# The chunk inversion of an RWKV-7 layer on 32x32 diagonal blocks in four partition quadrants, with one joining level

## The reference, cut to what matters

```python
def rwkv7_scan(r, w, k, v, kk, a, s0):
    def step(s, inp):
        r_t, w_t, k_t, v_t, kk_t, a_t = inp
        s_kk = jnp.einsum('bhvk,bhk->bhv', s, kk_t)
        s = (s * w_t[:, :, None, :] - s_kk[..., None] * (kk_t * a_t)[:, :, None, :]
             + v_t[..., None] * k_t[:, :, None, :])
        return s, jnp.einsum('bhvk,bhk->bhv', s, r_t)
```

## Time and profile before

| | |
|---|---|
| median of 3 runs | 4778.01 us (4769.5 to 4778.93) |
| the profiled execution | 4774.47 us |
| its span, first to last instruction | 4772.8 us |
| mean granted TensorE clock | 0.923 of 2.4 GHz |
| RWKV layers, inversion and chain | 371 to 998 us and 3829 to 4441 us |

### The profile page before, as it was taken

The page is one execution under the profiler, slowest core; times in us unless marked ns, Lnnn a source line. Parts: engine busy times, 40 slices in busy tenths (PEclk is TensorE's granted clock), DMA queues, the critical chain, the costliest instruction groups (busy, mean ns, idle before and its releaser), DMA issues.

```text
span 4772.8 us, 95942 instructions
## 1 busy us (share of the span) xinstructions
PE 4178.3 (88%) x37843; PEld 2571.5 (54%) x37843; DVE 2314.5 (48%) x4411; ACT 1370.2 (29%) x2518; POOL 525.5 (11%) x523
## 2 busy tenths in 40 slices
PE   4797999979999899978999885789997979999797
PEld 4346878844444344433444344444443468888676
DVE  5555555436652466633664215366623145555331
ACT  1004555421210355521221014222201045554230
POOL 0002323200000122210000000000000023232000
PEclk6898999989999899989999997899998979999899
DMA  4330000014432223213443210144421200000243
GB/s 147 97 117 26 4 4 4 3 40 135 148 116 86 69 91 95 89 44 101 141 141 101 71 59 0 35 127 141 128 84 54 83 19 3 4 4 4 83 133 109
DMA packets 475026, 350.75 MB, mean 73 GB/s; under 512 B 18016, under 2 KB 443176, under 8 KB 472520
## 3 DMA queue, kind: packets, MB, share of 16 engines
q1 hardware_dynamic: 449784, 240.11, 17.2%
q0 software_dynamic: 24912, 105.87, 6.2%
HBM read 344.76 MB, written 1.18 MB: 72 GB/s over the span
## 4 chain that ended last, share of the span: by engine, by line
PE 73%; DVE 13%; ACT 6%; issue 4%; DMA 4%; SPq 0%; DVEq 0%; ACTq 0%; POOLq 0%
PE PS L225 50%; PE PS L1417 18%; DMA WR<-in_ffn_w_in_dram 2%; PE PS L348 2%; DVE WORK L450 1%; DVE WORK L341 1%; DVE WORK L1169 1%; DVE WORK L1172 1%; DVE WORK L780 1%; PE PS L949 1%; DMA WR<-in_ffn_w_out_dram 1%; DVE H L453 1%; ACT WORK L1057 1%; ACT WORK L1654 0%; DVE BIG L1864 0%
## 5 line engine op out<-in xcount | busy, mean ns | idle before, releaser
L225 PE MATMUL PS<-H,WR 128*128 128x512 f32 (+1 forms) x3792 | 1519.5, 560 | 100.2 <-DVE WORK L540 37.8
L225 PEld LDWEIGHTS PS<-H,WR 128*128 128x128 f32 x3792 | 718.5, 192 | 859.4 <-issue 791.2
L225 PE MATMUL PS<-BIG,WR 128*128 128x512 f32 (+1 forms) x2592 | 1043.9, 564 | 92.8 <-DVE BIG L1818 59.2
L225 PEld LDWEIGHTS PS<-BIG,WR 128*128 128x128 f32 x2592 | 498.7, 194 | 625.5 <-issue 593.9
L341 DVE SCALAR_TENSOR_TENSOR WORK<-WORK,SC 128x512 f32<-128x512 f32 (+2 forms) x798 | 487.9, 611 | 28.5
L1417 PE MATMUL PS<-BIG,WORK 64*64 64x32 f32 (+1 forms) x9984 | 438.3, 224 | 61.4 <-DVE BIG L1924 60.0
L1417 PE MATMUL PS<-WORK,BIG 64*64 64x32 f32 (+1 forms) x8960 | 452.3, 227 | 23.8 <-DVE WORK L1928 12.9
L1417 PEld LDWEIGHTS PS<-BIG,WORK 64*64 64x64 f32 x9984 | 374.6, 140 | 90.2 <-issue 65.1
L1417 PEld LDWEIGHTS PS<-WORK,BIG 64*64 64x64 f32 x8960 | 370.9, 142 | 81.7 <-ACT WORK L1643 29.6
L579 DVE SCALAR_TENSOR_TENSOR X<-PS,MOD,X 128x256 f32 x112 | 54.2, 484 | 607.3 <-PE PS L225 598.4
L1772 POOL TENSOR_TENSOR WORK<-WORK,K 128x256 f32<-128x256 f32 x320 | 255.0, 797 | 788.4 <-ACT WORK L1643 396.9
(11 more groups left out here) (237 smaller groups left out, 4298.4 us busy)
## 6 DMA issues: line engine op xcount, KB each, us to landing
WR<-in_ffn_w_in_dram SPq DMA_DIRECT2D x176, 512.0 KB, 3.7
WORK<-in_ada_w_dram POOLq DMA_DIRECT2D x33, 2048.0 KB, 8.6
WR<-in_ffn_w_out_dram SPq DMA_DIRECT2D x64, 512.0 KB, 3.9
WR<-in_ssd_w_in_dram SPq DMA_DIRECT2D x48, 512.0 KB, 3.9
BIG<-scratch_dram POOLq DMA_DIRECT2D x8, 2048.0 KB, 7.9
BIG<-in_ada_w_dram SPq DMA_DIRECT2D x6, 2048.0 KB, 8.0
WORK<-in_ada_w_dram POOLq DMA_DIRECT2D x12, 1024.0 KB, 5.9
WR<-in_ffn_w_out_dram SPq DMA_DIRECT2D x32, 384.0 KB, 3.3
```

What stands on the lines that cost most here:

```text
L225: mm = pe.matmul(outs, WR[:, slot, k, 0:m], rhs(k), start=first and k == 0, stop=last and k == nk - 1)
```

## The change

The 64x64 matrix is first inverted on its two 32x32 diagonal blocks alone, and these lie one below the other on partitions: `QUADS[b][n]` is block b of head n, so four quadrants of 32 partitions hold two heads times two blocks. A matmul has 32 weight rows and 32 weight columns there and serves one quadrant, one chunk. `YX` holds both forms of the four chunks of one thread, 32 columns each; `NS` gets the off-diagonal 32x32 block of the product as well, which G makes on its own (10 matmuls a chunk in place of 4). The levels 2 to 16 run as before on these blocks: Z has 16 matmuls of 32 columns, X 32 of 16 columns.

A fifth step pair, m = `LAST`, joins the blocks. Z multiplies the off-diagonal block with the natural form of one diagonal block, with weights in one quadrant and the result in the other. X writes the whole 64x64 natural inverse into PSUM: both diagonal blocks by multiplying the transposed form with the identity, the off-diagonal one with Z, 24 matmuls, 8 of them of 64 columns. One VectorE copy of 256 columns takes it to `INV`, which no longer has a transposed form. The masks on GpSimd are four, of 128 columns, and the identity on ScalarE is written at the start of the own slot, since `YX` is shared by the thread before. Matmuls of the inversion: 8192 before, 16896 after; the chain, R, H and everything outside the RWKV layers stay.

```diff
-LEVELS = (2, 4, 8, 16, 32)
+LEVELS = (2, 4, 8, 16)
...
-HALF_CONST = ["id64", "id64", "pair0", "pair1", "lev2_0", "lev2_1", "lev4_0", "lev4_1", "lev8_0", "lev8_1",
-              "lev16_0", "lev16_1", "lev32_0", "lev32_1"]
+HALF_CONST = ["id64"]
+QUARTER_CONST = ["id32", "pair0", "pair1"] + [f"lev{n}_{d}" for n in (2, 4, 8, 16) for d in range(2)]
...
-        INV = work(4 * T).rearrange("p (d h c f) -> p d h c f", d=2, h=2, c=NQ)
-        G2, BK, G1R = by_chunk(P), by_chunk(P), by_chunk(Q)
+        INV, G2, BK, G1R = by_chunk(Q), by_chunk(P), by_chunk(P), by_chunk(Q)
+        YX = work(8 * Q).rearrange("p (d h c f) -> p d h c f", d=2, h=2, c=4)
         VTK = [work(T) for _ in range(2)]
-        sub = lambda: work(4 * Q).rearrange("p (c f) -> p c f", c=4)
-        NS = [sub() for _ in range(2)]
+        NS = [work(4 * Q).rearrange("p (o c f) -> p o c f", o=2, c=4) for _ in range(2)]
+        sub = lambda: work(4 * 32).rearrange("p (c f) -> p c f", c=4)
         OM = [[sub() for _ in range(2)] for _ in range(2)]
         ZB = [sub() for _ in range(2)]
-        ZB32 = [z[:, 0:2, :].rearrange("p c (h f) -> p (c h) f", h=2) for z in ZB]
         SIG, AA, RESET, PN = both_d(T), both_d(T), work(T), both_d(T)
         ARS = work(2048).rearrange("p (d n t) -> p d n t", d=2, n=2)
...
+        QUADS = [[slice(Q * n + 32 * b, Q * n + 32 * b + 32) for n in range(2)] for b in range(2)]
+        LAST = len(LEVELS)
...
-            for m in range(len(LEVELS)):
+            for m in range(LAST + 1):
                 inv += [(k, q, s, m) for k in "ZX" for q in both]
...
-            if h + 1 < SLOTS:
-                beside += [(22 + d, "I", 2 * ((h + 1) // 2) + d, (h + 1) % 2) for d in range(2)]
-            steps = [("I", d, 0) for d in range(2)] if h == 0 else []
+            steps = [("I", q, s) for q in both]
...
                 bank, removed = PS[:, 3 + d, :], AR[i % 2][:, d, 0, :]
+                half = lambda c, b: slice(ORDER_Q[d][4 * s + c] * Q + 32 * b, ORDER_Q[d][4 * s + c] * Q + 32 * b + 32)
                 for c in range(4):
-                    cs = tok(ORDER_Q[d][4 * s + c])
-                    for hs in HALF:
-                        last = mm(bank[hs, 4 * Q + c * Q:4 * Q + c * Q + Q], removed[hs, cs], AD[hs, d, cs])
-                done(last, f"{q}.gt{s}")
-                for c in range(4):
-                    cs = tok(ORDER_Q[d][4 * s + c])
-                    for hs in HALF:
-                        last = mm(bank[hs, c * Q:c * Q + Q], AD[hs, d, cs], removed[hs, cs])
+                    for b in range(2):
+                        for n, hs in enumerate(HALF):
+                            mm(bank[QUADS[b][n], c * 32:c * 32 + 32], AD[hs, d, half(c, b)], removed[hs, half(c, b)])
+                    for b in range(2):
+                        for n, hs in enumerate(HALF):
+                            mm(bank[QUADS[b][n], 256 + c * 32:256 + c * 32 + 32], removed[hs, half(c, b)], AD[hs, d, half(c, b)])
+                    b = 1 - d
+                    for n, hs in enumerate(HALF):
+                        last = mm(bank[QUADS[b][n], 384 + c * 32:384 + c * 32 + 32], removed[hs, half(c, b)],
+                                  AD[hs, d, half(c, 1 - b)])
                 done(last, f"{q}.g1{s}")
...
             def z_step(q, s, m):
-                d, n = q % 2, LEVELS[m]
-                pe.wait_ge(pool_done, C.at(f"{t}.{q}.om{s}{m}"))
+                d = q % 2
                 pe.wait_ge(vec_done, C.at(f"{t}.{q}.xx{s}{m - 1}") if m else C.at(f"{t}.{q}.xi{s}"))
+                if m < LAST:
+                    pe.wait_ge(pool_done, C.at(f"{t}.{q}.om{s}{m}"))
                 for c in range(4):
-                    y = INV[:, d, 0, 4 * s + c, :]
-                    o = slice(c * Q, c * Q + Q) if n < 32 else slice(c * 32, c * 32 + 32)
-                    for hs in HALF:
-                        last = mm(PS[hs, 3 + d, o], OM[d][m % 2][hs, c, :],
-                                  y[hs, :] if n < 32 else y[hs, 32 - 32 * d:64 - 32 * d])
+                    o = slice(c * 32, c * 32 + 32)
+                    if m < LAST:
+                        for b in range(2):
+                            for qs in QUADS[b]:
+                                last = mm(PS[qs, 3 + d, o], OM[d][m % 2][qs, c, :], YX[qs, d, 0, c, :])
+                    else:
+                        for to, qs in zip(QUADS[d], QUADS[1 - d]):
+                            last = mm(PS[to, 3 + d, o], NS[d][qs, 1, c, :], YX[qs, d, 0, c, :])
                 done(last, f"{q}.z{s}{m}")
 
             def x_step(q, s, m):
-                d, n = q % 2, LEVELS[m]
+                d = q % 2
                 pe.wait_ge(act_done, C.at(f"{t}.{q}.zc{s}{m}"))
-                bank = PS[:, 3 + d, 4 * Q:]
+                bank = PS[:, 3 + d, :]
+                if m == LAST:
+                    for c in range(4):
+                        o = 256 + c * Q
+                        for qs, own in zip(QUADS[d], QUADS[1 - d]):
+                            mm(bank[qs, o + 32 * d:o + 32 * d + 32], YX[qs, d, 1, c, :], quarter_const("id32")[qs, :])
+                            mm(bank[own, o:o + Q], YX[own, d, 1, c, :], half_const("id64")[own, :])
+                        for qs in QUADS[d]:
+                            last = mm(bank[qs, o + 32 - 32 * d:o + 64 - 32 * d], YX[qs, d, 1, c, :], ZB[d][qs, c, :])
+                    done(last, f"{q}.x{s}{m}")
+                    return
+                n = LEVELS[m]
                 for c in range(4):
-                    for hs in HALF:
-                        z = second(d, n)(ZB[d][hs, c, :]) if n < 32 else ZB32[d][hs, c, :]
-                        out = bank[hs, c * 32:c * 32 + 32]
-                        last = mm(blocks_of(out, n) if n < 32 else out, INV[hs, d, 1, 4 * s + c, :], z)
-                done(last, f"{q}.xy{s}{m}")
-                if n < 32:
-                    for c in range(4):
-                        for hs in HALF:
-                            last = mm(blocks_of(bank[hs, P + c * 32:P + c * 32 + 32], n), ZB[d][hs, c, :],
-                                      first(d, n)(INV[hs, d, 1, 4 * s + c, :]))
-                    done(last, f"{q}.x{s}{m}")
+                    for b in range(2):
+                        for qs in QUADS[b]:
+                            last = mm(blocks_of(bank[qs, P + c * 16:P + c * 16 + 16], n), YX[qs, d, 1, c, :],
+                                      second(d, n)(ZB[d][qs, c, :]))
+                for c in range(4):
+                    for b in range(2):
+                        for qs in QUADS[b]:
+                            last = mm(blocks_of(bank[qs, 192 + c * 16:192 + c * 16 + 16], n), ZB[d][qs, c, :],
+                                      first(d, n)(YX[qs, d, 1, c, :]))
+                done(last, f"{q}.x{s}{m}")
...
             def identity(q, s_):
-                if q >= 2:
-                    act.wait_ge(pe_done, C.at(f"{t}.{q - 2}.u{4 * s_ + 3}"))
-                eye = half_const("id64").unsqueeze(1).unsqueeze(1).broadcast_to([P, 2, 4, Q])
-                s(act.activation(INV[:, q % 2, :, 4 * s_:4 * s_ + 4, :], eye, ACT.Copy), f"{t}.{q}.id{s_}")
+                if q >= 2 or s_:
+                    q0, s0 = thread_before(q, s_)
+                    act.wait_ge(pe_done, C.at(f"{t}.{q0}.x{s0}{LAST}"))
+                eye = quarter_const("id32").unsqueeze(1).broadcast_to([P, 8, 32])
...
-                    act.wait_ge(pool_done, C.at(f"{t}.{q0}.om{s0}{len(LEVELS) - 1}"))
-                copy(NS[q % 2].rearrange("p c f -> p (c f)"), PS[:, 3 + q % 2, 4 * Q:], f"{q}.n{s_}")
+                    act.wait_ge(pe_done, C.at(f"{t}.{q0}.z{s0}{LAST}"))
+                copy(NS[q % 2].rearrange("p o c f -> p (o c f)"), PS[:, 3 + q % 2, 4 * Q:], f"{q}.n{s_}")
...
-                cols = 4 * Q if LEVELS[m] < 32 else 4 * 32
-                copy(ZB[q % 2].rearrange("p c f -> p (c f)")[:, 0:cols], PS[:, 3 + q % 2, 0:cols], f"{q}.zc{s_}{m}")
+                copy(ZB[q % 2].rearrange("p c f -> p (c f)"), PS[:, 3 + q % 2, 0:P], f"{q}.zc{s_}{m}")
...
-                lev = half_const(f"lev{LEVELS[m]}_{q % 2}").unsqueeze(1).broadcast_to([P, 4, Q])
-                g(pool.tensor_tensor(OM[q % 2][m % 2], NS[q % 2], lev, ALU.mult), f"{t}.{q}.om{s_}{m}")
+                lev = quarter_const(f"lev{LEVELS[m]}_{q % 2}").unsqueeze(1).broadcast_to([P, 4, 32])
+                g(pool.tensor_tensor(OM[q % 2][m % 2], NS[q % 2][:, 0, :, :], lev, ALU.mult), f"{t}.{q}.om{s_}{m}")
...
-                pair = lambda n: by4(half_const(f"pair{n}")).bitcast(mybir.dt.int32)
+                pair = lambda n: by4(quarter_const(f"pair{n}")).bitcast(mybir.dt.int32)
                 c4 = lambda ap: ap.rearrange("p (c f) -> p c f", c=4)
                 vec.wait_ge(act_done, C.at(f"{t}.{q}.n{s_}"))
-                v(vec.copy_predicated(half_inv(q, s_, 0), pair(d), c4(PS[:, 3 + d, 0:4 * Q])))
```

(22 more changed lines are left out.)

22 lines of the change are left out of this document (15 added, 7 removed).

## The result

| | before | after |
|---|---|---|
| median | 4773.8 us (4 runs) | 5030.9 us (5027.3 to 5041.2, 4 runs) |
| ratio | | 1.0542, 95% interval 1.052 to 1.0563 |
| span of the profiled execution | 4772.8 us | 5025.6 us |
| instruction packets (queue q8) | 252 | 388 |

The changed kernel is 257 us slower. The forecast was +52 us (4830), in the range but far from its middle; the cause of most of the loss was in none of its terms.

What follows compares the result with a forecast made beforehand. It took the RWKV layers to be bound by TensorE's rate of small matmuls, priced by weight loads. Matmuls -152, shape changes +164, clock +60 and neighbours -20 gave +52 us, forecast 4830 us; 8-in-10 range 4725 to 5060.

Steps and rivals of the forecast that it cites:

- Matmuls, -152 us: Inversion in both RWKV layers: 264 lighter matmuls a thread replace 128, saving 2.4 us on each of 64 threads.
- That a matmul of 32 columns costs no less leaves the weights as the price: Z and X steps before: 58 ns a matmul for 64 or 32 streamed columns, so weight loading sets the price.
- The 16 ns: Price per 32x32 matmul in Z and X of the first four levels, four quadrants at once; 3.1 us a thread.
- SyncE's queue and the DMAs are as before, but for the instructions themselves: 4 and 4 GB/s.: Both RWKV layers: queue and DMA traffic unchanged except for instructions; no time booked.
- Changes of shape, +164 us: TensorE array in both RWKV layers: 1214 more changes of shape at 0.135 us each; ends +109 and +212 us.
- The row at 631.76: Trace before, 631.76 to 633.09 us: 0.98 us of work in 1.33, read as two shape changes of 0.175 us each.
- The lower bound of 0.09: Least price of a shape change, in us: the array empties and no weight load is exposed.
- Clock, +60 us: TensorE in both RWKV layers: thinner stream lengthens 1.2 GHz stretches by 125 us, at half price; ends 0 and +150.
- Neighbours, -20 us: VectorE, ScalarE and GpSimd work beside the inversion: shorter copies and gaps falling in waits; range 0 to -60 us.
- The fourth, a price per matmul: Inversion matmuls keep costing 58 ns each, +505 us instead of -152; 5485 us in all, chance 0.07.
- The second rival, faster: Four quadrants at once, shape changes only 0.09 us, clock unchanged, copies give 40: 4695 us, half effect 4740; chance 0.20.
- The third's number, 5075 us: Array overlaps only two neighbouring matmuls at a time: +75 us for matmuls, +300 in all; chance 0.17.

Runs made afterwards that it cites:

- the stream: Changed kernel plus dependence-free matmuls behind layer 0's RWKV stage, 512 of 32x32 weights over four quadrants written out; fastest blocks 3.48 us per 256 instructions.
- The run with fat islands: Changed kernel with Z matmuls streaming 64 columns instead of 32 and X 32 instead of 16, same instruction count and order; 5040.5 us, ratio 1.0553.
- the control: Kernel before with 640 added 64x64 matmuls in their neighbours' shape, compared with 640 of 32x32 that change shape; 4799.6 us (1.0044) against 4876.1 us (1.0214).
- wider streams: Kernel before with X matmuls of the first four levels streaming 64 columns instead of 32; 4764.3 us in fp32, 4705.2 us in bf16.

## Why the prediction was wrong, step by step

The step that failed is the supply of instructions, which was put at nothing: the trace has 184 us of stops for it. The terms that were booked came out near in sum, +72 us of running time against 102 measured, -20 of waits against -32, though single ones did not.

**Matmuls, -152 us.** The rate inside a step was right: 0.38 and 0.65 us to the next step for Z and X, four quadrants at once. The counts were right. What the working missed stands behind "That a matmul of 32 columns costs no less leaves the weights as the price": the 58 ns were put down to the load of 64 weight columns, and lighter weights were then booked at 16 ns. The load is what the array needs, but the instruction supply needed 54 ns a matmul in the stream's fastest blocks and lay 4 ns beneath it, hidden. The 16 ns, bounded from bursts of under 1 us, were then used as if they held for a whole layer. By the stage tables, both layers held 28256 matmul records, 221 blocks, at 3.48 us 768 of 1239 us; now they hold 45664, 357 blocks, 1241 of 1491 us. In the kernel before that bound was slack, in the changed one it is 83% of the stage. Bursts pay before the mean does: 125 of the 166 intervals between stops are one block or two, though the mean block of the layer takes 4.2 us (1491/357).

**"SyncE's queue and the DMAs are as before, but for the instructions themselves: 4 and 4 GB/s."** This is the step that failed: the one sentence that named the cause dismissed it by bandwidth. The supply is no matter of bandwidth: of the three parts 1.16, 0.92 and 1.40 us two pass without any packet, and the DMA share over the whole block is 0.02. In its place stand 184 us of stops, 166 of 168 ending 1.2 to 1.6 us behind a packet.

**Changes of shape, +164 us.** Measured 0.064 us each in the kernel's time, so +78, and 0.092 in TensorE's running time. The row at 631.76 has two changes to and from 128 columns, with an exposed load, and no change between 64 and 32; which of its costs do not come back there was not taken apart. The lower bound of 0.09 stands in the prediction without a row. It fits TensorE's own time, but not the kernel's, because part of a change lies in waits.

**Clock, +60 us.** Half-clock time rose by 405 us, not 125; at half price that would be 200, out of the term's range. The run with fat islands took 243 us of it away for nothing, but its Z steps cost more and its stops grew, so it does not show that the clock cost nothing. What the term measures stays open. The running time leaves room for it: 102 us is all three terms together, so with -152 and 0.092 for each of 1214 changes some 142 us remain for the clock and for what else was booked too low.

**Neighbours, -20 us.** The durations came as booked. The gaps at semaphore waits fell by 32 us; how much of that is the shorter copies' doing was not measured apart.

The forecast missed by 205 us (257 less 52). Of these 184 are the stops, a mechanism without a term; the other 21 are, but for a few, the balance of the booked ones.

**Rivals.** The fourth, a price per matmul, had a chance of 0.07 and was nearest to the mechanism. It was argued per record and within a step, where the trace disproves it: some 8 ns a load. The Trainium skill's 25 ns between starts of matmuls (TensorE: Matmul & The Clock Gate, "Wait — 56ns, not 53.3ns?"), with which it was weighed, does not hold over four quadrants either: a Z step passes its 32 matmul records in 0.38 us, 12 ns each. It is also not what the supply sets, which is 3.48/128 = 27 ns a record as a mean over a block. The second rival, faster, was wrong for the same reason as the forecast, though it was right that part of a change lies in waits. The third's number, 5075 us, was close by accident: all four quadrants loaded at once.

## What to carry to other kernels

Where a stretch of straight-line code has small instructions, count instructions beside time: here 256 of TensorE's instructions took 3.3 us at the least and 3.48 in a steady stream, so an fp32 matmul of four was worth some 54 ns there although its tile needed 16, and splitting a matmul into smaller ones that run side by side paid nothing beyond that. Before a tile is cut up, look how close the present rate is to that bound; what helped here was fewer instructions (bf16 took two for a matmul instead of four), and a short loop brought no packets at all. In a trace, look for gaps before instructions that wait for no semaphore, a multiple of 256 instructions apart.

## What the runs showed of the hardware

- A block of 256 instructions of straight-line code costs 3.3 us at the least between two stops of the changed kernel and 3.47 to 4.03 us in the stream, where its packet takes 0.92 to 1.45; 166 of 168 stops end 1.2 to 1.6 us after a packet has landed. In a loop of 16 matmuls no packet was moved and a matmul took 32 ns.
- Four 32x32 quadrants side by side load at some 8 ns a load at 2.4 GHz, 13 ns at 1.2 GHz. X is as fast with 32 streamed columns as with 16; Z with 64 columns took 0.49 us for its 32 loads, with 32 columns 0.34.
- A change between 64x64 and 32x32 shape costs 0.064 us of the kernel's time and 0.09 us of TensorE's. The Trainium skill (TensorEngine Tiling (Array Packing), "Key Properties") says that changing the tiling mode drains the array. That a change costs time in the control agrees with it.
- 640 additional matmuls of 64x64 in the kernel before cost 39 ns each and lowered its half-clock time from 215 to 165 us; wider streams lowered it as well, and the time gained 12 us at the most from it.
